# Seven block products of 256 tokens in place of eight for half of the first stage's values

## The reference

```python
def chunked_sgu_mixer(h, w_in, ln_w, ln_b, w_s, b_s, w_out):
    z = h @ w_in                       # h: 512 x 1024, w_in: 1024 x 6144
    u, v, g = jnp.split(z, 3, axis=-1)
    u = jax.nn.gelu(u)
    v = layer_norm(jax.nn.gelu(v), ln_w, ln_b)      # v: 512 x 2048
    ...
    s = jnp.einsum('gts,bnsgc->bntgc', w_causal, v) + b_s.T[None, None, :, :, None]
    y = u * s.reshape(B, S, A_WIDTH) * jax.nn.silu(g)
    return y @ w_out
```

## Time and profile before

| | |
|---|---|
| time, median of 3 runs | 1831.31 us (1829.69 to 1831.59) |
| time of the profiled execution | 1829.83 us |
| its span | 1827.7 us |
| granted TensorE clock, mean | 0.997 |
| TensorE busy | 1792.5 us of the span |
| stage `a_v`, rounds 4 to 7 | from 54.99 to 100.28 us |

### The profile page before, as it was taken

How to read it: one execution, slowest core, us unless ns; L and a number is a source line. 1 busy time by engine, 2 the same in 40 slices (tenths; PEclk the granted TensorE clock), 3 DMA queues, 4 the chain that set the end, 5 groups by cost and what they waited for, 6 DMA issues and landing times.

```text
span 1827.7 us, 28330 instructions
## 1 busy us (share of the span) xinstructions
PE 1792.5 (98%) x10236; PEld 1528.0 (84%) x10236; DVE 1126.0 (62%) x1741; ACT 710.5 (39%) x1337; POOL 1286.9 (70%) x1190
## 2 busy tenths in 40 slices
PE   9999999999999999999999999999999998999998
PEld 7888888878878899998888877798876778999886
DVE  5166774149984798887016767574454189888731
ACT  3111111127762366552014267553413255666001
POOL 7766666767777798877667865453772687888775
PEclk9999999999999999999999999999999999999999
DMA  5222223232223323235223311201321222323421
GB/s 187 94 91 92 92 92 138 92 120 78 89 69 116 131 100 103 106 109 189 95 92 104 103 60 47 69 26 47 116 95 44 93 110 76 115 96 113 165 101 69
DMA packets 25886, 179.36 MB, mean 98 GB/s; under 512 B 2864, under 2 KB 2992, under 8 KB 6704
## 3 DMA queue, kind: packets, MB, share of 16 engines
q1 hardware_dynamic: 24048, 168.31, 26.0%
q10 hardware_dynamic: 1728, 9.58, 1.4%
HBM read 171.58 MB, written 6.29 MB: 97 GB/s over the span
## 4 chain that ended last, share of the span: by engine, by line
PE 84%; DVE 8%; ACT 3%; issue 3%; POOL 1%; DMA 1%; DVEq 0%; ACTq 0%; POOLq 0%
PE bank L457 12%; PE bank L458 12%; PE bank L459 12%; PE bank L1216 6%; PE bank L1218 6%; PE bank L1217 6%; PE bank L1666 2%; PE bank L1667 2%; PE bank L1668 2%; PE bank L495 2%; PE bank L496 2%; PE bank L497 2%; DVE temps L1397 1%; PE bank L2071 1%; PE bank L2347 1%
## 5 line engine op out<-in xcount | busy, mean ns | idle before, releaser
L350 POOL TENSOR_TENSOR weights_lo<-raw_weights,weights_hi 128x512 fp32r<-128x512 f32 (+4 forms) x416 | 558.8, 1343 | 41.2 <-ACT weights_hi L369 7.4
L348 POOL TENSOR_SCALAR weights_hi<-raw_weights 128x512 fp32r<-128x512 f32 (+4 forms) x392 | 268.0, 684 | 340.1 <-PE bank L459 173.7
L457 PE MATMUL bank<-x_hi,weights_hi 128*128 128x512 f32 x688 | 271.5, 395 | 0.2
L459 PE MATMUL bank<-x_lo,weights_hi 128*128 128x512 f32 x688 | 267.9, 389 | 0.0
L458 PE MATMUL bank<-x_hi,weights_lo 128*128 128x512 f32 x688 | 267.8, 389 | 0.0
L457 PEld LDWEIGHTS bank<-x_hi,weights_hi 128*128 128x128 f32 x688 | 129.2, 188 | 28.1 <-POOL weights_lo L350 0.8
L459 PEld LDWEIGHTS bank<-x_lo,weights_hi 128*128 128x128 f32 x688 | 129.1, 188 | 27.1
L458 PEld LDWEIGHTS bank<-x_hi,weights_lo 128*128 128x128 f32 x688 | 129.2, 188 | 26.9 <-issue 1.0
L1218 PE MATMUL bank<-x_lo,weights_hi 128*128 128x256 f32 x432 | 122.2, 283 | 0.0
L1258 POOL TENSOR_TENSOR weights_lo<-temps,weights_hi 128x512 fp32r<-128x512 f32 x72 | 108.1, 1521 | 2.7 <-ACT weights_hi L1290 2.7
L1258 POOL TENSOR_TENSOR weights_lo<-raw_weights,weights_hi 128x512 fp32r<-128x512 f32 x72 | 97.6, 1360 | 13.3 <-ACT weights_hi L1290 13.0
(11 more groups left out here) (552 smaller groups left out, 5076.6 us busy)
## 6 DMA issues: line engine op xcount, KB each, us to landing
raw_weights<-in_ffn_seven SPq DMA_DIRECT2D x36, 1024.0 KB, 4.7
raw_weights<-in_a_ug SPq DMA_DIRECT2D x16, 1024.0 KB, 4.8
raw_weights<-in_b_in SPq DMA_DIRECT2D x12, 1024.0 KB, 4.8
raw_weights<-in_ffn_down SPq DMA_DIRECT2D x12, 1024.0 KB, 4.7
raw_weights<-in_ffn_down SPq DMA_DIRECT2D x7, 1408.0 KB, 6.2
raw_weights<-in_a_out SPq DMA_DIRECT2D x8, 1024.0 KB, 4.8
raw_weights<-in_ffn_up SPq DMA_DIRECT2D x8, 1024.0 KB, 4.8
raw_weights<-in_a_v SPq DMA_DIRECT2D x7, 1024.0 KB, 4.8
```

The source lines that it names most:

```text
L348: nc.gpsimd.tensor_scalar(hi, raw, 1.0, 0.0, ALU.mult, ALU.add).then_inc(S("units_hi"), 1)
L350: nc.gpsimd.tensor_tensor(lo, raw, hi.bitcast(F32), ALU.subtract).then_inc(units_ready, 1)
L457: nc.tensor.matmul(ps, wh, xh[:, k, :], start=k == 0, stop=False)
L459: last = nc.tensor.matmul(ps, wh, xl[:, k, :], start=False, stop=k == last_k)
```

## The change

The last two column blocks of `v` (512 tokens, 1024 columns, k = 1024: rounds 4 to 7 before) are cut into halves of tokens, columns and k, and made from seven products in place of eight, by the scheme of Winograd. `a_v` has 4 rounds left. A product is 256 tokens (two banks) by 512 columns by 512 of k: 4 units of 6 matmuls. Its token side is either a part of `x_hi`/`x_lo` or one of four mixtures of quarters of x, its weight side either a block as loaded (`B11`, `B12`, `B21`, `B22`: `src[4]` to `src[7]`) or one of four running differences of blocks.

- ACT gets eight copies of x times the norm weight (`v_mixed`) and four copies of mixtures to fp32r, ahead of the copy of bank 6. DVE gets four subtractions or additions that make the mixtures and four that make their low parts, each 128 x 1024, behind `dve_lru_cols`.
- In the seven products the high part of a unit is made by ACT (`act_v_hi`), the low part by POOL for three units of four and by DVE for the fourth (`low`). DVE makes 16 differences of units (`summed`), in place in the block buffers. A product's slots are freed by `av_used`.
- M1, M6, M7 and M4 are accumulated one over the other in banks 2 and 3; after M1, M6 and M7 ACT copies the banks out (`act_v_keep`). M5 and then M2 use banks 0 and 1, M3 uses banks 4 and 5. DVE adds the kept parts (`joined`, 8 instructions), and ACT applies the gelu to each finished block.
- The mask of `a_w_s` comes one round earlier on POOL, and the sums of `a_w_s` go to banks 6 and 7, between M2 and M7.
- Two block buffers are filled by DMAs of their own, and the first loads of `a_ug` wait for the last uses of the blocks.

```diff
-    Phase("a_v", 8, 16), Phase("a_ug", 16, 16), Phase("a_out", 8, 16),
+    Phase("a_v", 4, 16), Phase("a_ug", 16, 16), Phase("a_out", 8, 16),
...
+        def sp_v_blocks(sp):
+            src = dram["a_v"]
+            sp.dma_start(flat(V_B11), src[4]).then_inc(S("av_b11"), 16)
+            sp.dma_start(flat(V_B22), src[7]).then_inc(S("av_b22"), 16)
+            sp.wait_ge(units_ready, PH["a_v"].used(3, 3))
+            sp.dma_start(flat(V_B12), src[6]).then_inc(S("av_b12"), 16)
+            sp.wait_ge(units_ready, PH["a_v"].used(2, 3))
+            sp.dma_start(flat(V_B21), src[5]).then_inc(S("av_b21"), 16)
...
+        def pool_v_lows(pool):
+            for n, p in enumerate(V_ORDER):
+                for j in range(3):
+                    hi, lo = v_weights(j)
+                    pool.wait_ge(*due("av_hi", 4 * n + j + 1))
+                    nc.gpsimd.tensor_tensor(lo, v_unit(V_FROM[p], j), hi.bitcast(F32), ALU.subtract).then_inc(S("av_lo"), 1)
...
+            def product(p, banks, opens):
+                n = V_ORDER.index(p)
+                xh, xl, first_k, half = V_X[p]
+                for j in range(4):
+                    wh, wl = (flat(w) for w in v_weights(j))
+                    v_low_ready(pe, n, j)
...
+            pe.wait_ge(*due("a_v_free", TOK))
+            product("M1", V_Z, True)
+            pe.wait_ge(*due("av_mixed_lo", 1))
+            product("M5", V_C11, True)
+            pe.wait_ge(*due("av_kept", 2))
+            pe.wait_ge(*due("av_mixed_lo", 3))
+            product("M6", V_Z, False)
+            pe.wait_ge(*due("av_kept", 4))
+            product("M2", V_C11, True)
...
+            pe.wait_ge(*due("av_kept", 6))
+            product("M7", V_Z, False)
+            pe.wait_ge(*due("av_mixed_lo", 4))
+            product("M3", V_C12, True)
+            pe.wait_ge(*due("av_kept", 8))
+            product("M4", V_Z, False)
...
         def act_a_v(act):
...
+            for k in range(KD):
+                nc.scalar.activation(V_MIX[:, k, :], A_X[:, k, :], ACT.Copy, scale=vec("norm0", k)).then_inc(S("av_gained"), 1)
+            for t in V_MIX_PART:
+                act.wait_ge(*due("av_mixed", t))
+                nc.scalar.activation(v_part(V_MIX_H, t), v_part(V_MIX, t), ACT.Copy).then_inc(S("av_mixed_hi"), 1)
+            act.wait_ge(*due("s0_diag", 1))
+            act.wait_ge(units_used, PV.used(1, 3))
+            act_rows(act, "s0", PS[6], RB[:, :])
...
         def dve_a_v(dve, step):
...
+            for i in range(TOK):
+                stats(i, 0, i + 1)
+            low(0)
+            dve.wait_ge(*due("av_b12", 16))
+            for j in range(4):
+                v_low_ready(dve, 0, j)
+                summed(0, j, V_B11, V_B12, V_B11)
+            dve.wait_ge(*due("av_b22", 16))
+            for j in range(4):
+                if j == 3:
+                    low(1)
+                v_low_ready(dve, 1, j)
+                dve.wait_ge(*due("av_sums", j + 1))
+                summed(4, j, V_B11, V_B22, V_B11)
+            for i in range(TOK):
+                stats(i, 1, TOK + i + 1)
+            low(2)
+            for j in range(4):
+                summed(8, j, V_B12, V_B22, V_B12)
+            dve.wait_ge(*due("av_b21", 16))
+            for j in range(4):
+                v_low_ready(dve, 2, j)
+                dve.wait_ge(*due("av_sums", 4 + j + 1))
+                summed(12, j, V_B11, V_B21, V_B11)
+            low(3)
+            low(4)
...
```

More of the change, by code:

```diff
@@ L339, in split_unit @@
                     wait(pool, units_used, PH["fox_v"].used(1, j))
+            elif ph.name == "a_ug" and first(r):
+                pool.wait_ge(*due("av_used", V_UNITS - 4 + j + 1))
             elif not (isinstance(r, int) and ph.base + r == 0):
@@ new lines, in v_part, with v_unit, v_weights, v_low_ready @@
+        def v_part(tile, t):
+            k, tok = V_MIX_PART[t]
+            return tile[:, k, tok]
+        def v_unit(block, j):
+            return block[:, 4 * j:4 * j + 4, :]
+        def v_weights(j):
+            return WH[:, SLOT[j]:SLOT[j] + 4, :], WL[:, SLOT[j]:SLOT[j] + 4, :]
+        def v_low_ready(eng, n, j):
+            if j < 3:
+                eng.wait_ge(*due("av_lo", 3 * n + j + 1))
+            else:
+                eng.wait_ge(*due("av_lo_by_dve", n + 1))
+        def pool_v_lows(pool):
[4 more added lines that the diff above has]
+                    nc.gpsimd.tensor_tensor(lo, v_unit(V_FROM[p], j), hi.bitcast(F32), ALU.subtract).then_inc(S("av_lo"), 1)
@@ new lines, in pe_v_sevens @@
+        def pe_v_sevens(pe):
+            def product(p, banks, opens):
[4 more added lines that the diff above has]
+                    v_low_ready(pe, n, j)
+                    for i, bank in enumerate(banks):
+                        at = half * SEQ // 2 + i * P
+                        tok = slice(at, at + P)
+                        nc.tensor.matmul(bank, xh[:, first_k + j, tok], wh, start=opens and j == 0, stop=False, skip_group_check=True)
+                        nc.tensor.matmul(bank, xh[:, first_k + j, tok], wl, start=False, stop=False, skip_group_check=True)
+                        last = nc.tensor.matmul(bank, xl[:, first_k + j, tok], wh, start=False, stop=j == 3, skip_group_check=True)
+                    last.then_inc(S("av_used"), 1)
+            pe.wait_ge(*due("a_v_free", TOK))
[7 more added lines that the diff above has]
+            product("M2", V_C11, True)
+            pe.wait_ge(*due("ws_causal", 1))
+            pe.wait_ge(*due("a_v_free", 2 * TOK))
+            for half in range(2):
+                nc.tensor.matmul(PS[6 + half], ONES[:, :], A_WS[:, 4 * half:4 * half + 4, :].rearrange("p g t -> p (g t)"), start=True, stop=True).then_inc(S("ws_sums"), 1)
+            pe.wait_ge(*due("av_kept", 6))
[4 more added lines that the diff above has]
+            product("M4", V_Z, False)
@@ L704, in free @@
                 def free(i):
-                    if pair >= 2:
-                        pe.wait_ge(*due("a_v_free", 4 * (pair - 2) + i + 1))
-                    elif pair == 1 and i == 2:
+                    if pair == 1 and i == 2:
                         pe.wait_ge(*due("s0_rb", 1))
@@ L714, in pe_a_v @@
                     pe_spread(pe, "s0", DIAG, PS[6])
[L715 to L719, removed]
-        def act_a_v(act):
[L722 to L733, removed]
@@ new lines, in pe_a_v, with act_v_gelu, act_v_hi @@
+            pe_v_sevens(pe)
+        def act_v_gelu(act, src, i, block):
+            nc.scalar.activation(A_V[:, i, block * SEQ:(block + 1) * SEQ], src, ACT.Gelu_apprx_tanh, scale=COL[:, i:i + 1]).then_inc(S("a_v_free"), 1)
+        def act_v_hi(act, n, j):
+            p = V_ORDER[n]
+            if n == 0:
+                act.wait_ge(units_used, PV.used(3, j))
+            else:
+                act.wait_ge(*due("av_used", 4 * (n - 1) + j + 1))
+            if p in V_SUM_AT:
+                act.wait_ge(*due("av_sums", V_SUM_AT[p] + j + 1))
+            elif j == 0:
+                act.wait_ge(*due({"M1": "av_b11", "M2": "av_b21", "M3": "av_b22"}[p], 16))
+            hi, _ = v_weights(j)
+            nc.scalar.activation(hi, v_unit(V_FROM[p], j), ACT.Copy).then_inc(S("av_hi"), 1)
@@ L735, in dve_a_v, with stats @@
         def dve_a_v(dve, step):
             BN = T[:, 5, 0:96].rearrange("p (t b s) -> p t b s", t=TOK, s=6)
[L739 to L744, removed]
+            def stats(i, block, count):
+                dve.wait_ge(*due("a_v_free", count))
+                step(nc.vector.bn_stats(BN[:, i, block, :], A_V[:, i, block * SEQ:(block + 1) * SEQ]))
@@ new lines, in dve_a_v @@
+            for i in range(2):
+                joined(V_C11[i], V_C11[i], V_KEPT1[i])
+            dve.wait_ge(*due("av_kept", 6))
+            for i in range(2):
+                joined(V_U2[i], V_U2[i], V_KEPT5[:, i, :])
+            for i in range(2):
+                stats(i, 2, 2 * TOK + i + 1)
+            low(5)
+            dve.wait_ge(*due("av_kept", 8))
+            for i in range(2):
+                joined(V_U3[i], V_U3[i], V_KEPT5[:, i, :])
+            low(6)
+            dve.wait_ge(*due("av_used", 24))
@@ L745, in dve_a_v @@
+            dve.wait_ge(*due("av_joined", 4))
+            for i in range(2):
+                joined(V_C12[i], V_C12[i], V_U2[i])
+            for i in range(2):
+                stats(2 + i, 3, 2 * TOK + 3 + i)
+            for i in range(2):
+                stats(i, 3, 2 * TOK + 5 + i)
+            for i in range(2):
+                stats(2 + i, 2, 2 * TOK + 7 + i)
             for i in range(TOK):
```

116 lines of the change are left out of this document (106 added, 10 removed).

## The result

The changed kernel takes 1844.6 us (median of 4 runs, 1844.2 to 1845.5) against 1831.0 us before on the same chip (1829.7 to 1831.6): a ratio of 1.0074, 95% interval 1.0061 to 1.0087. The profiled execution took 1845.0 us, 15.1 more than that of before (15.5 more by the span). First the page: busy time by engine, and the chain that ended last by engine.

A forecast was written before the change was run, and what follows sets the result against it. TensorE, busy 98% of the span, was taken to bound the kernel. The terms 7.8 + 1.7 - 5.4 + 10.2 + 1.7 - 0.4 = +15.6 us on 1829.8 gave 1845.4, stated as 1846, range 1838 to 1851 (8 in 10).

The forecast's parts named there:

- the likeliest case: Whole kernel: the forecast of 1846 us itself, with its own range 1842 to 1849; chance 72%.
- wait in round 2: Round 2, third token tile: TensorE waits for ACT's copy of bank 6, held behind DVE's mixtures; 7.8 us, bounds 6.7 to 9.6.
- clock behind it: Behind the round 2 wait: granted clock falls, mostly to half level; 1.7 us, as after a profiled wait of 3.25.
- 24 matmuls less: Rounds 4 to 7: seven products of 24 matmuls replace 192 matmuls at 0.2267 us each; 5.4 us less.
- DVE and POOL up to `low(3)`: Seven products: DVE and POOL run one at a time, so TensorE waits 10.2 us in all; bounds 0 to 11.8.
- clock behind M2's wait: Behind the long wait at M2's fourth unit: the clock drops once more, costing 1.7 us.
- tail: Ahead of the first spatial product: TensorE's 0.28 us gap and slow restart go; 0.4 us less.
- S: The start of M1, from which the times in the seven products are counted; `low(3)` was put at S + 30.5 us.
- Three waits, 3, 1 and 6 us: Seven products: the 10.2 us shows as waits at the fourth units of M5 (3), M6 (1) and M2 (6).
- The rival on the other side: Faster than before: DVE's two-operand instructions run freely beside POOL throughout; even this mechanism alone leaves +2.6 us; chance 3%.
- the first rival: Seven products: the port costs little, so the 10.2 us and second clock drop go; +3.7 us, 1833.5 to 1835; chance 8%.

The follow-up runs named there:

- The run with the copy first: Changed kernel with ACT's copy of bank 6 moved ahead of the four high parts of the mixtures; 1835.4 us, ratio to before 1.0028.
- the run in which nothing waits: Changed kernel with the copy of bank 6 ahead of the high mixtures and the 16 differences' second operand in PSUM; 1824.6 us, ratio 0.9962.
- the run with PSUM operands: Changed kernel, second operand of DVE's 16 differences read from PSUM bank 4 (last 1024 columns wrong); 1834.4 us; with copy of bank 6 first too, 1824.6.
- the fastest one that computes everything: Changed kernel with bank 6 copy first, `low(1)` first, M4's differences late, and `low(3)` ahead of M7's last difference; 1825.9 us, ratio 0.9972.
- the runs with the mask back: Changed kernel with POOL's mask of `a_w_s` moved back behind round 3; 1844.1 us, ratio 1.0076.
- the run with the statistics last: Changed kernel: bank 6 copy and `low(1)` first, M4's differences late, block 1 statistics behind all differences, `low(3)` before M7's last; 1829.0 us, ratio 0.9988.

## Why the prediction was right

1846 was forecast and 1844.6 measured, and the likeliest case is the one that happened. Its terms against the trace, for the profiled execution:

| term | forecast | measured |
|---|---|---|
| wait in round 2 | +7.8 | +7.5 |
| clock behind it | +1.7 | +2.7 |
| 24 matmuls less | -5.4 | -5.4 |
| DVE and POOL up to `low(3)` | +10.2 | +8.7 |
| clock behind M2's wait | +1.7 | +1.8 |
| tail | -0.4 | -0.4 |
| sum up to the first spatial product | +15.6 | +14.8 |

The measured terms are rounded and add up to 14.9. The total is nearer than its parts: 1.0 us too little for the clock and 1.5 too much for DVE and POOL partly cancel, which is luck.

- *Wait in round 2*: right in place, cause and size. ACT's first high mixture waited for DVE's mixtures, which began at 35.47 (35.7 forecast) and took 4.99 (5.0). The run with the copy first took away this wait with the clock behind it, and only these.
- *Clock behind it*: mis-sized. I took over the 1.7 us of a wait of 3.25 us. Here the clock had already fallen before TensorE went on at 42.08 and stood at the half level until about 47.5. M1 started 10.16 us late; the third token tile, at 42.08 in place of 34.58, was 7.5 late. The rest is 2.7.
- *24 matmuls*: exact. In the run in which nothing waits the stage is 168 x 0.2267 us and the sums of `a_w_s`, 39.85 us.
- *DVE and POOL up to low(3)*: the cause was right, as the run with PSUM operands showed, and the size 1.5 us too high. `low(3)` ended at 94.21, S + 29.1 against S + 30.5. DVE's statistics go back to back at 0.72 us (2.87 for four), where I took 0.96 from rows in which they wait for ACT: 1.0 too much. The other 0.5 is what remains for POOL's 12 low parts when DVE's 20 instructions are put at 0.60, 13.3 us in place of 13.8. None of the low parts fell beside the statistics, though I had counted on one, so each cost DVE about 1.1 us and not 1.26.
- *Three waits, 3, 1 and 6 us*: two were seen, 2.24 and 4.35. M6's did not exist: `low(2)` ended at 82.26, and TensorE at full clock would have been there at 82.6. Behind M5's wait the clock fell for 3.4 us, 1.7 us lost, and as forecast this was absorbed, since M2's wait became that much shorter: 2.24 + 4.35 and the clock and slow restart between them are 8.7.
- *Clock behind M2's wait*: from 94.26 to 115.47 are 21.2 us, where 72 + 6 matmuls and the sums take 19.4: 1.8.
- *Tail*: right; 0.28 us of wait and the slow restart are gone.

The rival on the other side, DVE running freely beside POOL, is answered by the PSUM run too: with that alone the time is 1834.4, inside what the first rival gave (1833.5 to 1835). That is 3.0 above its own before, where I had +2.6 for this mechanism alone. It needed the copy of bank 6 moved as well to end faster than before.

So the loss was not the scheme's. Its gain, 5.8 us forecast, came out whole once TensorE did not wait (6.8 in the run with PSUM operands, 5.4 in the fastest one that computes everything); 10 us were lost by the place of one ACT instruction, and 10 by DVE and POOL taking turns.

## What to carry to other kernels

Before new work is put into an engine's queue, look for the instruction behind it that the bottleneck waits for, and let that go first: here a copy of 0.6 us behind four mixtures cost 10 us. Where DVE and GpSimd both work out of SBUF, add their times as for one engine whenever DVE has two SBUF operands, give such work one operand in PSUM, or lay GpSimd's instructions beside DVE's single-operand ones. Ahead of a deadline put only what the deadline needs, but look at who waits for what is put off: the statistics moved back cost 3 us elsewhere.

## What the runs showed of the hardware

- The clock does not follow from a wait's length alone. A wait of 2.24 us in the changed kernel was followed by a fall to the half level a microsecond after TensorE had gone on, for 3.4 us. The same wait in the runs with the mask back and with the copy first was followed by a fall too, 0.6 and 0.2 us after TensorE had gone on. Behind one of 2.08 us, in the run with the statistics last, the granted clock stayed at 1.00. The clock behind the waits of 7.46 and 4.35 us cost 2.7 and 1.8 us. What sets 2.24 and 2.08 us apart is open.
- A two-operand DVE instruction of 128 x 8 took 1.00 us beside POOL's mask and 0.17 without it. It started 0.11 us behind the mask and ended with it, at 35.54 against 35.52, so what it paid here was the rest of POOL's instruction and not a share by its own size.
